# One decoder-layer step on one core: host-side layouts for x, y, keys, values and u in place of transposes on the chip

## The reference, cut to what matters

```python
q, k, v, hc, bc, cc = split(rms_norm(x, g_mix) @ w_in)      # 2048 -> 6 x 1024
q, k = rms_norm(q), rms_norm(k)                             # over each head's 64
u = cc * hc                                                 # input of the short convolution
attn = dilated_attention(q, k, v, rel_bias)                 # prompt: a sum of 3 dilations
                                                            # sample: 256 cached rows and the new one
cat = [rms_norm(attn), rms_norm(bc * conv3(u))]
h = x + cat @ w_out
h = h + (silu(n @ w_gate) * (n @ w_up)) @ w_down            # n = rms_norm(h)
y = h + sigmoid(rms_norm(h) @ w_ple_gate) * (p @ w_ple_proj)
# outputs: y, the new keys k and values v, the last two rows of u, the old and new u of the samples
```

## Time and profile before

| what | us |
|---|---|
| median of 3 runs | 2585.83 (2585.45 to 2592.28) |
| the profiled execution, its own time | 2585.61 |
| its span, first to last instruction | 2584.1 |
| PE busy, PEld busy | 2516.5, 2497.8 |
| DVE busy | 1751.8 |
| ACT busy | 950.2 |
| POOL busy | 286.9 |

### The profile page before, as it was taken

One profiled execution on the slowest core, in us unless ns is written; L12 is line 12 of the kernel. 1 busy time (PEld: TensorE's weight loads), 2 busy tenths in 40 slices (PEclk: granted clock), 3 DMA queues, 4 the chain that ended last, 5 costly groups with the idle time before them and its releaser, 6 DMA issues.

```text
span 2584.1 us, 52528 instructions
## 1 busy us (share of the span) xinstructions
PE 2516.5 (97%) x20677; PEld 2497.8 (97%) x20677; DVE 1751.8 (68%) x2181; ACT 950.2 (37%) x1283; POOL 286.9 (11%) x335
## 2 busy tenths in 40 slices
PE   8898999999989989999999999999999999999998
PEld 7898999999989979999999999999999999999998
DVE  3566777777686879889888898888433322466332
ACT  5333333343342444444444444444322211233221
POOL 2111111111021000000000000000000000142101
PEclk9999999999999989999999999999999999999999
DMA  6544333434344344445444454444665543233331
GB/s 194 159 114 126 107 112 103 122 106 113 99 127 132 118 115 115 134 130 145 130 114 133 129 144 130 114 134 130 209 207 173 159 141 116 80 89 101 107 109 58
DMA packets 482496, 328.31 MB, mean 127 GB/s; under 512 B 19382, under 2 KB 458714, under 8 KB 481400
## 3 DMA queue, kind: packets, MB, share of 16 engines
q1 hardware_dynamic: 451936, 250.74, 34.6%
q0 software_dynamic: 28848, 75.06, 9.0%
q10 hardware_dynamic: 1648, 1.65, 0.2%
HBM read 286.80 MB, written 44.91 MB: 128 GB/s over the span
## 4 chain that ended last, share of the span: by engine, by line
PE 88%; DMA 4%; DVE 4%; ACT 2%; issue 2%; POOL 0%; SPq 0%; ACTq 0%; DVEq 0%; POOLq 0%
PE acc L552 16%; PE acc L556 16%; PE acc L554 16%; PE acc L779 11%; PE acc L778 11%; PE acc L780 11%; DMA wraw<-in_w_in 2%; DMA wraw<-in_w_down 1%; ACT whi L924 1%; PE aux L594 1%; DVE wlo L1297 1%; PE aux L562 1%; DMA x_nat<-in_x_prompt 1%; PE aux L638 1%; PE aux L567 0%
## 5 line engine op out<-in xcount | busy, mean ns | idle before, releaser
L1297 DVE TENSOR_TENSOR wlo<-wraw,whi 128x1024 fp32r<-128x1024 f32 (+1 forms) x276 | 332.5, 1205 | 424.9 <-ACT whi L924 424.2
L924 ACT ACTIVATE whi<-wraw 128x1024 fp32r<-128x1024 f32 (+1 forms) x276 | 285.2, 1034 | 704.9 <-PE acc L556 593.4
L778 PE MATMUL acc<-xb_hi,whi 128*128 128x260 f32 x1232 | 349.2, 283 | 12.4 <-DVE xb_lo L1655 12.4
L779 PE MATMUL acc<-xb_lo,whi 128*128 128x260 f32 x1232 | 349.5, 284 | 0.0
L780 PE MATMUL acc<-xb_hi,wlo 128*128 128x260 f32 x1232 | 348.9, 283 | 0.0
L780 PE MATMUL acc<-xa_hi,wlo 128*128 128x260 f32 x1232 | 348.7, 283 | 0.0
L779 PE MATMUL acc<-xa_lo,whi 128*128 128x260 f32 x1232 | 348.5, 283 | 0.0
L778 PE MATMUL acc<-xa_hi,whi 128*128 128x260 f32 x1232 | 348.4, 283 | 0.0
L552 PE MATMUL acc<-slots_a,whi 128*128 128x260 f32 x1536 | 315.0, 287 | 0.0
L556 PE MATMUL acc<-slots_a,wlo 128*128 128x260 f32 x1536 | 310.2, 283 | 0.0
L554 PE MATMUL acc<-slots_a,whi 128*128 128x260 f32 x1536 | 308.4, 282 | 0.0
(11 more groups left out here) (308 smaller groups left out, 5099.7 us busy)
## 6 DMA issues: line engine op xcount, KB each, us to landing
wraw<-in_w_in SPq DMA_DIRECT2D x96, 512.0 KB, 4.0
blocks<-in_w_gate SPq DMA_DIRECT2D x88, 512.0 KB, 6.3
blocks<-in_w_up SPq DMA_DIRECT2D x88, 512.0 KB, 6.2
wraw<-in_w_down SPq DMA_DIRECT2D x48, 448.0 KB, 3.8
wraw<-in_w_out SPq DMA_DIRECT2D x32, 512.0 KB, 3.9
wraw<-in_w_ple_gate SPq DMA_DIRECT2D x32, 512.0 KB, 4.0
slots_b<-f_dram SPq DMA_DIRECT2D x28, 520.0 KB, 4.8
f_dram<-sig_t POOLq DMA_DIRECT2D x22, 520.0 KB, 3.3
```

The costliest lines, as they stand in the source:

```text
L778: mm(to, w_h, hi[:, n, X_OF[u], :], start=p == 0, stop=False)
L779: mm(to, w_h, lo[:, n, X_OF[u], :], start=False, stop=False)
L924: on(whi[:, u % HILO, 0:width], wraw[:, u % RAW, 0:width], ACT.Copy).then_inc(s_whi, 1)
L1297: V.tensor_tensor(wlo[:, u % HILO, 0:width], wraw[:, u % RAW, 0:width], whi[:, u % HILO, 0:width].bitcast(F32), ALU.subtract).then_inc(s_w ...
```

## The change

The kernel's inputs and outputs change their layouts, and the host makes and undoes them. x comes twice: as tiles `x_tiles` (128 x 16 x 520) and, for the squares alone, as rows of tokens as before. p, the conv state and all gains come as tiles and columns. y, k, v and the last ten columns of u are stored as they are held. So PE transposes only v, four pieces a pair. Two things come with it:

- In the first pair ACT squares x between the splits of units 4 to 7, and the inverse root is taken on the 128x4 sums before they are spread.
- Where the conv half of `w_out` begins, PE does seven of the eight blocks of two units before it needs the last conv tile; the norm's sums are taken as columns, inverted small and then spread; attention of the last pair runs one unit later; DVE moves `v_lo`, the taps and q's norm.

The start:

```diff
-START_SPLITS = (2, 8, 13, 15)
+START_SPLITS = (1, 8)
...
         def load_x(g):
-            at_g = slice(g * XP * P, (g + 1) * XP * P)
-            sp.dma_start(x_nat[:, :, at_g], x_prompt[0, :, at_g].rearrange("(b p) f -> p b f", p=P)
-                         ).then_inc(l_x[g], 16)
+            sp.dma_start(hid[:, g * XP:(g + 1) * XP, :], x_tiles[:, g * XP:(g + 1) * XP, :]).then_inc(l_x[g], 16)
```

PE, `heads(j, a, g)`:

```diff
             if g == 10:
                 if a is not None:
                     pe.wait_ge(s_pt2, 8 * a + 8)
-                    pe.wait_ge(s_o, 2 * a + 2)
+                else:
+                    pe.wait_ge(s_vk, 2)
                 pe.wait_ge(s_read, 6 * j + 3)
-                nc.tensor.transpose(aux[0:DEC, BANK_O, 0:P], v_t[:, SEQ:T], ident[:, :])
                 for b in range(QB):
                     done = nc.tensor.transpose(aux[:, BANK_T, b * P:(b + 1) * P], v_t[:, b * P:(b + 1) * P], ident[:, :])
                 done.then_inc(s_nat, 1)
-            if g == 11:
...
-                nc.tensor.transpose(aux[0:DEC, BANK_O, P:2 * P], k_t[:, SEQ:T], ident[:, :])
-                nc.tensor.transpose(aux[0:DEC + 2, BANK_O, 2 * P:3 * P], u_t[:, SEQ:SEQ + 2 + DEC], ident[:, :])
-                for b in range(QB):
-                    done = nc.tensor.transpose(aux[:, BANK_T, b * P:(b + 1) * P], k_t[:, b * P:(b + 1) * P], ident[:, :])
-                done.then_inc(s_nat, 1)
```

PE, in the first pair, after unit 4:

```diff
-                    pe.wait_ge(s_cp0, 5)
-                    pe.wait_ge(s_xsq, QB + 1)
+                    pe.wait_ge(s_bias, 1)
+                    pe.wait_ge(s_ninv, N_X)
```

PE, the conv half of `w_out`:

```diff
+        for i in range(2):
+            pe.wait_ge(s_read, T_CONV + i - 1)
+            unit(at, i, mixed, range(KC - 1), i, True, False, (s_x, KT + 1) if i == 0 else None, signal=False)
+        unit(at, 0, mixed, (KC - 1,), 0, False, True, (s_x, KT + KC), n0=KC - 1)
...
+        unit(at, 1, mixed, (KC - 1,), 1, False, True, n0=KC - 1)
+        pe.wait_ge(s_ninv, N_CONV)
```

ACT, `heads`, g = 10; at g = 11 the copies (lines 1003 to 1005) and their waits are gone:

```diff
-                act.wait_ge(s_nat, 2 * j + 1)
-                if a is not None:
-                    act.wait_ge(d_v, 16 * j)
-                    act.wait_ge(d_k, 16 * j)
-                    act.wait_ge(d_small, 64 * j)
-                on(v_nat[:, :, :], aux[:, BANK_T, :].rearrange("p (b f) -> p b f", b=QB), ACT.Copy).then_inc(s_natsb, 1)
...
+                on(vhi[:, :, :], aux[:, BANK_T, :].rearrange("p (b f) -> p b f", b=QB), ACT.Copy).then_inc(s_vhi, 1)
```

ACT, `pair`:

```diff
+                if a is None and g < QB:
+                    square_x(g)
+                if a is None and g == QB - 1:
+                    first_root()
...
         def square_x(b):
+            act.wait_ge(l_xn[b], 16)
```

DVE, before `v_t`, `k_t` and `u_t` are written again:

```diff
+                    dve.wait_ge(d_v, 16 * j)
...
-                    dve.wait_ge(s_nat, 2 * j)
+                    dve.wait_ge(d_k, 16 * j)
...
+                if a is not None:
+                    dve.wait_ge(d_u, 16 * j)
```

DVE, y:

```diff
-                V.tensor_tensor(y_t[:, :], res[:, 1, :], hid[:, m, :], ALU.add).then_inc(s_y, 1)
+                V.tensor_tensor(hid[:, m, :], res[:, 1, :], hid[:, m, :], ALU.add).then_inc(s_y, 1)
```

POOL:

```diff
             if fresh:
-                pool.wait_ge(d_skew, 16 * KA)
+                pool.wait_ge(d_skew, 16 * 4)
...
+            pool.dma_start(v_tiles[:, bass.ds(j, 1), :].squeeze(1), v_t[:, :]).then_inc(d_v, 16)
...
+            pool.dma_start(k_tiles[:, bass.ds(j, 1), :].squeeze(1), k_t[:, :]).then_inc(d_k, 16)
...
+            pool.dma_start(u_tail[:, bass.ds(j, 1), :].squeeze(1), u_t[:, SEQ:T + 2]).then_inc(d_u, 16)
...
+        for g in range(PIECES):
+            pool.wait_ge(l_x[g], 16)
+        for b in range(QB):
+            pool.dma_start(x_nat[:, b, :], x_prompt[0, b * P:(b + 1) * P, :]).then_inc(l_xn[b], 16)
         pool.wait_ge(s_xsq, QB + 1)
         load_keys(0)
...
-        for n in range(4):
+        for n in range(1, 4):
             pool.wait_ge(s_unit, 4 + n)
-            pool.dma_start(xt_dram[:, n * 4:(n + 1) * 4, :], hid[:, n * 4:(n + 1) * 4, :]).then_inc(d_spill, 16)
-        for n in range(1, 4):
-            pool.wait_ge(s_unit, 6 + 2 * n)
             store_skew(2 * n, 2 * n + 2)
```

SP, the last store:

```diff
-        sp.wait_ge(s_ycp, KT * 2 - 1)
+        sp.wait_ge(s_y, KT * 2)
+        sp.dma_start(y_tiles[:, KT - 1, :], hid[:, KT - 1, :]).then_inc(d_last, 16)
```

More of the change, by code:

```diff
@@ L535, in _, with unit @@
         mm = nc.tensor.matmul
-        def unit(at, u, operand, tiles, slot, first, last, ready=None, between=None):
+        def unit(at, u, operand, tiles, slot, first, last, ready=None, between=None, n0=0, signal=True):
             pe.wait_ge(s_wlo, at.count(u))
@@ L1425, in heads @@
                 V.memset(u_t[:, 0:2], 0.0).then_inc(s_pad, 1)
-                dve.wait_ge(s_nroot, N_X)
-                V.reciprocal(rstd[:, :], rstd[:, :]).then_inc(s_ninv, 1)
-                dve.wait_ge(s_ninv, N_X)
-                dve.wait_ge(s_read, 2)
-                for tile in (v_t, k_t):
-                    V.tensor_tensor(tile[:, :], tile[:, :], rstd[:, :], ALU.mult).then_inc(s_vk, 1)
             if g == 1:
@@ L1512, in pair @@
             for g in range(PAIR_UNITS):
-                split(at, g + HILO)
+                if not (last and g == PAIR_UNITS - 1):
+                    split(at, g + HILO)
                 if a is not None:
@@ L1519, in pair @@
                         conv_lo(c)
+            if last:
+                conv_lo(KC - 1)
+                split(at, PAIR_UNITS - 1 + HILO)
+                norm_q(KA - 1, KA - 2)
         def conv_lo(c):
@@ L1991, in _ @@
         pair(0, fresh=True)
+        pool.wait_ge(d_skew2, 64)
         with pool.Fori(1, KA - 1) as a:
@@ L2106, with rows @@
     got = run(nc, [arrays], core_ids=[0]).results[0]
-    return tuple(got[f"out_{n}"] for n in outs)
+    def rows(name):
+        a = got[f"out_{name}"]
+        return np.ascontiguousarray(a.transpose(2, 1, 0).reshape(a.shape[2], -1))
+    y, k, v, u = rows("y_tiles"), rows("k_tiles"), rows("v_tiles"), rows("u_tail")
+    conv_sample = np.stack([got["out_old_passed"], u[2:]], axis=1)
+    return (y[None, :SEQ], y[SEQ:, None], k[:SEQ].reshape(1, 1, SEQ, HEADS, HD), v[:SEQ].reshape(1, 1, SEQ, HEADS, HD),
+            u[None, None, :2], k[SEQ:].reshape(1, DEC, 1, HEADS, HD), v[SEQ:].reshape(1, DEC, 1, HEADS, HD),
+            conv_sample[None])
```

491 lines of the change are left out of this document (185 added, 306 removed).

## The result

The changed kernel takes 2556.06 us (median of 4 runs, 2555.98 to 2558.73), the kernel before 2585.64 in the same comparison: a ratio of 0.9887, with a 95% interval of 0.9872 to 0.9903. It is 29.6 us faster. The forecast was 2537, with a range up to 2553; so some 19 us of the gain are missing. The profiled execution, the slowest of the four, took 2558.73 us with a span of 2557.2.

The account below looks back on a forecast made before the run. PE with its weight load, busy 97% of the span, was taken to bound the kernel. Terms 3.1 + 8.1 + 1.1 + 1.9 + 10.5 + 9.1 + 9.4 + 5.3 = 48.5 us took 2585.6 to 2537.1; range 2525 to 2553.

Parts of the forecast that it names:

- Steady pairs: Pairs 3 to 6: transposes leave PE, 0.77 us a pair, 3.1 us in all; step between sums of g = 9 is 84.0 us.
- y: Output tiles of y: five transposes a tile leave PE, 0.54 us each of 15 times between matmuls, 8.1 us.
- p: Ten transposes of p leave PE at a 0.11 us pitch, 1.1 us.
- the start of the last store: Tail: SP can start the last store of y at about 2575.1 instead of 2577.02, 1.9 us.
- The start: Start of the kernel: unit 5 begins at 54 instead of 58.8 and unit 8's wait goes; 9.4 us, bounds 2 and 15.
- The chain behind: ACT's work from the split of unit 4 to the roots (splits, squares, reads, table load), some 17 us.
- weights flowing beside x: Rival, chance 0.2: unit 4's weights land at 30, the start gives 15 us, pair 2 keeps no wait; 2529.
- Pair 1: PE's 7.5 us wait, 2.2 of slow clock and 0.8 of transposes go; 10.5 us, bounds 7 and 12.
- Pair 2: The 10.3 us excess and 0.8 of transposes go, less 2.0 of wait kept; 9.1 us, bounds 4 and 11.
- The conv half: Third unit begins at 739.7 instead of 745.32, 17 us after pair 7 ends; 5.3 us, bounds 2 and 7.
- stores hold DVE: Rival, chance 0.03: v's store lands after DVE wants v's tile, in all seven pairs; 2594.5 if a store takes 25 us.
- The early waits stay under another name: Rival, chance 0.22: squares hold PE longer (start gives 2), pair 2 keeps 5 us and its slow clock (gives 4); 2549.

Follow-up runs that it names:

- e5_later: The changed kernel with the first bias store issued only after the squares of x; 2546.73 us, ratio 0.9846 to the kernel before.
- e6_knat: The kernel before, with ACT copying k for its store into a buffer of its own, so it no longer waits for v's store; 2580.15 us, ratio 0.9972.
- e4_onelate: The changed kernel with the bias of heads 8 to 15 stored by one DMA of 2 MB in pair 1 instead of four stores; 2551.50 us.
- e7_squares: e5_later with ACT squaring all of x and taking the roots ahead of the split of unit 4; 2557.66 us, ratio 0.9890 to the kernel before.

## Why the prediction was wrong

**What PE itself was relieved of was right.** Steady pairs 84.00 us, y 8.1, p near 1.1, the start of the last store 2.1. Here a count of instructions and a pitch from the timeline were enough, since there PE was busy throughout.

**The start failed, by 10.6 us.** The step was: "the weights of unit 4 at 31.5 + 4 = 35.5". They came at 47.9. I had taken the end of x as rows for all engines together and a landing in idle times for the weights. In fact about two engines, those that the first bias store had held, were still at work from 41 to 47 us, when the others had ended, and the load landed only when its last packets had passed there, one for each big packet. The load was issued at 28.4 and took 19.5 us. e5_later, without the store, brings it at 41.7: so the store accounts for 6.2 us of the 12.4. The other 6.2 go with x as rows. It was issued from 24.2 us on, not near 20, and filled the engines from about 26 to 38 us: the 11.5 us of the sum were right, its start was not. That part is read from the trace; no run takes it apart.

The earlier trace rows were read wrongly as well. The two loads of that window were issued at 62.1 and 63.7 us and sent no packet before 66; they landed after 7.3 and 8.5 us. SP's 45 packets were the end of an earlier load, so the share of 1.2% measured loads that had not started, not how weights move beside big packets.

The chain behind was sized well (15.7 us measured to the root, 17 taken). Weights as late as this were in neither bound. The rival of weights flowing beside x was wrong in its time; the turns that it rests on are there, but turns are not equal bytes.

**Pair 1 was right in size (9.0 for 10.5) and wrong in cause.** The step was: "ACT no longer copies k for an output, so it doesn't wait for v's store ... So the 7.5 us go". e6_knat shows that without this wait the weights hold ACT for 11.35 us instead: the row named the store, for which ACT stood first in its order, and the weights landed 0.4 us behind it. That the size came out was luck. What mattered, as far as runs show it, was the bias stores moved earlier (3.9 of the 9.0 us), to which I gave no term, and the copies of x that made room for them; 0.8 are transposes, and the cause of the rest stays open.

**Pair 2 failed by 3.8 us.** The cause was right (e6_knat gives 8.0 of it), and so was what stays, the weights beside the last bias store. It was mis-sized: 3.49 us of wait for the 2.0 that I kept, and a granted clock of 0.83 in the 10 us behind it, for which I had no term. e4_onelate recovers all of it. One thing I overlooked: in the kernel before POOL waited until the last bias store had landed before it loaded the next pair's bias, and that load took 3.9 us. In the changed kernel it goes out directly behind the store, at 186.5, and both ran beside the weights that were late:

```profile
skew<-skew_dram POOLq DMA_DIRECT2D x1, 512.0 KB, 18.2
```

These weights landed 7.9 us after unit 24 began, and 6.3 us after it before. No run takes this load apart from the store.

**The conv half failed by 5.4 us.** The third unit was said to begin 17 us after pair 7 ends, and it was 20.5. The sum itself was not complete: its terms, 11.5 of matmuls and waits of 2.7 and 1.6, make 15.8, so 1.2 stood for all else, and all else took 2.8. The order of DVE's steps was as I listed it, but they took longer. The split of 1.2 us took 2.33 and PE waited 4.6 and 1.6 us for the 2.7 and 1.6 of the sum:

```profile
715.88 2.33 DVE L1172 TENSOR_TENSOR wlo<-wraw,whi 128x1024 fp32r<-128x1024 f32 x1
718.14 3.39 DVE L1393 RECIPROCAL tmp<-tmp 128x520 f32<-128x520 f32 x1
...
723.65 0.17 DVE L1450 RECIPROCAL gsq<-gsq 128x4 f32<-128x4 f32 x1
```

So the third unit began 2.1 us sooner after pair 7 than before, where 5.6 were taken, and units 98 to 108 gave 2.4 back, to the slow clock behind the new waits: windows of the changed kernel (span, busy and count of five engines, granted clock, DMA share, GB/s) show 0.72 from 726 to 735 us.

```profile
726.00:735.00 9.00, 8.18 (x52) 8.19 (x53) 6.67 (x10) 0.16 (x1) 1.08 (x2) 0.72 0.53 154
```

**The rivals.** No row of the changed kernel has DVE waiting for `out_v_tiles`, and the slowest of these stores landed in 14.2 us, inside the 16.8; *stores hold DVE* is out. *The early waits stay under another name*, forecast as 2549, comes nearest, with 2556 against it: a wait for a DMA did stay at the start and in pair 2 (-1.2 and 5.3 us for its 2 and 4). But what held the start was late weights, not the squares that it named.

## What to carry to other kernels

When a removed wait had a late transfer beside it, take the wait away in thought and ask what the same engine would have waited for next; here it was the weights, which landed 0.4 us behind the store. Loads of weights issued just behind a bias store, which uses only two engines, took 12 to 16 us here where 4.0 is the median, so a DMA that uses few engines is worth widening or moving out of the way first; here that was worth 4.6 and 9.3 us. Freeing an engine early can start DMAs that cost more than it gave, as e7_squares did.

## What the runs showed of the hardware

Two queues on the same DMA engines moved equal numbers of packets in 4 us, 335 and 335, with sizes nearly eight times apart (1.31 and 0.17 MB).

VectorE ran slower beside GpSimd: seven operations L1180 of 128x520 took 6.63 us in the changed kernel while POOL did its squares and sums, from 703.4 to 706.6 us. Five of the seven took 0.75 us each; the two that lay beside POOL's took 1.55 and 1.80. POOL and DVE:

```profile
703.41 1.51 POOL L1757 TENSOR_TENSOR gsq<-hid 128x520 f32 x1 [6.69 <-DVE hid L1266]
705.00 1.64 POOL L1759 TENSOR_TENSOR sums<-sums,gsq 128x520 f32<-128x520 f32 x1
```

```profile
703.25 6.63 DVE L1180 SCALAR_TENSOR_TENSOR slots_c<-hid,cols,slots_c 128x520 fp32r<-128x520 f32 x7
```

Seven such operations in the start of the same trace (22.37 to 27.1 us), where POOL does no arithmetic, took 4.78 us.
